# Moving every large tile of a fused two-block kernel onto 512-byte or 1024-byte starts

## The reference

```
h = modulate(rms_norm(x, g_norm1), shift1, scale1)
proj = h @ w_in                                   # 1024 x 3088
...
x = x + (1 + gate1) * (mixed @ w_out)             # 1024 x 1024
u = causal_depthwise_conv(h2 @ w_up, w_conv, b_conv)   # 1024 x 5632
val, gte = split(u)
x = x + (1 + gate2) * ((val * silu(gte)) @ w_down)     # 2816 x 1024
...
def swiglu(h, w_gu, w_down):                      # layers two and three
    gate, up = split(h @ w_gu)
    return (silu(gate) * up) @ w_down
```

## Time and profile before

| | |
|---|---|
| time, median of 3 | 1083.9 us (1081.49 to 1085.06) |
| span of the profiled execution | 1082.7 us; its own time is not listed apart from the three |
| TensorE matmul busy | 1042.9 us, 96% of the span, 9968 matmul records |
| VectorE busy | 734.7 us, 68% |
| ScalarE busy | 562.1 us, 52% |
| transfers | 185.82 MB, 172 GB/s on average |
| granted TensorE clock, mean | 0.985 of full speed |

### The profile page before, as it was taken

One profiled execution on the slowest core, in us unless ns is written; L12 is line 12 of the kernel. 1 busy time (PEld: TensorE's weight loads), 2 busy tenths in 40 slices (PEclk: granted clock), 3 DMA queues, 4 the chain that ended last, 5 costly groups with the idle time before them and its releaser, 6 DMA issues.

```text
span 1082.7 us, 22912 instructions
## 1 busy us (share of the span) xinstructions
PE 1042.9 (96%) x9968; PEld 988.3 (91%) x9968; DVE 734.7 (68%) x1194; ACT 562.1 (52%) x858; POOL 0.9 (0%) x7
## 2 busy tenths in 40 slices
PE   7999999899999999998899999999999999999997
PEld 6798898899999998887779999999989799999996
DVE  3788658799976667887546566566757665556554
ACT  4446374666556448754236444454667655444431
POOL 0000000000000000000000000000000000000000
PEclk8999999899999999999999999999999999999999
DMA  9968455466645653331005555456224435554441
GB/s 348 393 216 312 176 195 204 153 228 237 232 148 176 220 224 118 118 118 42 4 2 170 196 187 187 140 182 222 100 74 155 175 119 195 188 183 149 173 166 39
DMA packets 31236, 185.82 MB, mean 172 GB/s; under 512 B 3472, under 2 KB 4768, under 8 KB 13984
## 3 DMA queue, kind: packets, MB, share of 16 engines
q1 hardware_dynamic: 31136, 184.36, 47.4%
HBM read 183.29 MB, written 1.05 MB: 170 GB/s over the span
## 4 chain that ended last, share of the span: by engine, by line
PE 88%; DVE 5%; ACT 3%; DMA 2%; issue 1%; SPq 1%; DVEq 0%; ACTq 0%
PE banks L361 48%; PE banks L1354 17%; PE banks L341 5%; PE banks L358 2%; PE banks L637 2%; DMA land<-in_mkv_a 1%; DVE wlo L321 1%; PE banks L1538 1%; PE banks L1897 1%; PE banks L1887 1%; PE banks L572 1%; DVE adac L556 1%; PE banks L640 1%; PE banks L1864 1%; DMA raw<-in_w_in 1%
## 5 line engine op out<-in xcount | busy, mean ns | idle before, releaser
L321 DVE TENSOR_TENSOR wlo<-raw,whi 128x2048 fp32r<-128x2048 f32 (+3 forms) x163 | 323.1, 1983 | 172.5 <-ACT whi L306 171.7
L306 ACT ACTIVATE whi<-raw 128x2048 fp32r<-128x2048 f32 (+3 forms) x163 | 270.5, 1661 | 109.3 <-PE banks L1354 78.0
L361 PE MATMUL banks<-h_hi,whi 128*128 128x256 f32 x1376 | 181.1, 283 | 1.3 <-ACT h_hi L987 1.2
L361 PE MATMUL banks<-h_lo,whi 128*128 128x256 f32 x1376 | 179.2, 281 | 0.7 <-DVE h_lo L1062 0.7
L361 PE MATMUL banks<-h_hi,wlo 128*128 128x256 f32 x1376 | 177.4, 281 | 0.0
L361 PEld LDWEIGHTS banks<-h_hi,whi 128*128 128x128 f32 x1376 | 169.1, 189 | 4.7 <-issue 2.5
L361 PEld LDWEIGHTS banks<-h_lo,whi 128*128 128x128 f32 x1376 | 167.4, 187 | 4.1 <-issue 2.6
L361 PEld LDWEIGHTS banks<-h_hi,wlo 128*128 128x128 f32 x1376 | 167.8, 188 | 1.6 <-issue 1.2
L1380 ACT ACTIVATE u<-u 128x256 f32<-128x256 f32 x44 | 18.4, 418 | 128.9 <-DVE u L1434 128.8
L1354 PE MATMUL banks<-m_lo,whi 128*128 128x256 f32 x528 | 75.4, 281 | 0.0
L1354 PE MATMUL banks<-m_hi,wlo 128*128 128x256 f32 x528 | 75.3, 281 | 0.0
(11 more groups left out here) (449 smaller groups left out, 1405.2 us busy)
## 6 DMA issues: line engine op xcount, KB each, us to landing
raw<-in_ada SPq DMA_DIRECT2D x24, 1024.0 KB, 6.2
raw<-in_w_up SPq DMA_DIRECT2D x22, 1024.0 KB, 4.8
raw<-in_a_gu SPq DMA_DIRECT2D x22, 1024.0 KB, 4.8
raw<-in_b_gu SPq DMA_DIRECT2D x22, 1024.0 KB, 4.9
raw<-in_w_in SPq DMA_DIRECT2D x12, 1024.0 KB, 7.1
raw<-in_w_down SPq DMA_DIRECT2D x16, 704.0 KB, 4.1
raw<-in_a_in SPq DMA_DIRECT2D x11, 1024.0 KB, 5.6
raw<-in_a_down SPq DMA_DIRECT2D x16, 704.0 KB, 4.1
```

Of the source, the lines that this page charges most:

```text
L306: act.activation(hi_s[k % NSPLIT][:, 0:w], raw[n % NRAW][:, 0:w], ACT.Copy).then_inc(*hi_made.tick(k))
L321: dve.tensor_tensor(lo_s[s][:, 0:w], raw[n % NRAW][:, 0:w], hi_s[s][:, 0:w].bitcast(F), SUB).then_inc(*lo_made.tick(k))
L361: i_ = pe.matmul(b[0:m, j * T:(j + 1) * T], a[:, kt * step + j * m:kt * step + j * m + m], x[:, kt, :], start=st, stop=sp)
```

## The change

No instruction is added, removed or moved: each engine's list of instructions before and after differs in line numbers alone. What differs is where tiles start. Four pads that nobody reads or writes take up 64, 96, 480 and 992 bytes of a partition, and `one` is allocated behind `masks` instead of ahead of it.

```diff
         vec = sb("vec", [P, NVEC])
         con = sb("con", [P, NCON])
+        sb("pad_low", [P, 16])
         raw = [sb(f"raw{i}", [P, SLOT]) for i in range(NRAW)]
         hi_s = [sb(f"whi{i}", [P, SLOT], R) for i in range(NSPLIT)]
         lo_s = [sb(f"wlo{i}", [P, SLOT], R) for i in range(NSPLIT)]
         X = sb("X", [P, 8, T])
+        sb("pad_high", [P, 120], side="right")
         early = ExitStack()
...
         adac = sb("adac", [P, 2, 2, P])
+        masks = sb("masks", [P, 7, P], R)
         one = sb("one", [P, 1])
-        masks = sb("masks", [P, 7, P], R)
...
         oma = sb("oma", [P, 6])
+        sb("pad_mid", [P, 24])
...
         gdec = sb("gdec", [P, 8], F, sc)
+        sb("pad_mix", [P, 248], F, sc)
         S1 = sb("S1", [P, 2, 4, 256], F, sc)
```

## The result

The changed kernel takes **1098.1 us**, the median of four executions (1097.2 to 1099.5). The kernel before took 1082.7 us beside it (four executions, 1080.9 to 1085.1). The recorded ratio is 1.0131, with a 95% interval from 1.0106 to 1.0156 (the two medians alone divide to 1.0142): slower by 1.3%, where 2.3% faster was forecast, and outside the range.

What follows compares the result with a forecast made beforehand. TensorE, busy 96% of the span, bounds; at 113.3 ns h saves 15.4 us, m 8.5, L358 0.9, others 1.8: 26.6, times 0.96 is 25.5, 1082.7 to 1057.2, forecast 1059 (own range 1054 to 1064; stated range 1046 to 1090).

Steps and rivals of the forecast that it cites:

- nothing changes: Rival for the whole kernel: excess is weight-load handover, addresses do not matter; 1084 us (1081 to 1087), chance 0.17.
- The moving tile: TensorE's matmuls: moving tiles on multiples of 128 bytes allow the quicker pace, 113.3 ns against 116.67 (h) and 118.69 (m).
- The upper bound: Slowest pace allowed for matmuls at the new starts: m's 118.69 ns, for everything.
- The weight load: TensorE's weight loads: 16 or 64 columns also give 117.5 ns, so the excess belongs to the moving side.
- the slower rival: Equal remainders bring moving and weight streams into step, locking all stretches at m's pace: 1088 to 1096 us, chance 0.18.
- Shortening TensorE by 3% leaves both idle: Layer two's up-projection: VectorE, busy 68.69 of 117 us, and ScalarE, 53.57, would not swallow the gain.
- mixed paces: Rival: some matmul stretches lock at 113.3 ns, others at 118.1; 1063 to 1078 us, chance 0.15.
- four fifths fast: Case of the mixed-paces rival with four fifths at the quick pace, over 6,700 matmuls: 1064 us.

Runs made afterwards that it cites:

- one pad of 32 bytes: The kernel before with only h's tiles moved by 32 bytes, making h's difference to the weights 0 modulo 256: 1095.1 us, ratio 1.0109.
- The streams by themselves: Separate kernels, no part of the reference: streams of 32 matmuls at chosen tile starts; 120.0 ns per matmul at difference 0, 113.3 at 192 in the first.
- the three pads: The kernel before plus pads of 96, 32 and 224 bytes, putting all moving tiles 192 from the weights modulo 256: 1069.1 us, ratio 0.9879, lowest median.

## Why the prediction was wrong

**What held.** TensorE is the bound, traffic isn't the excess, and the address reaches the pace: the rival "nothing changes" is refuted by one pad of 32 bytes. VectorE's and ScalarE's times don't see the remainder, float32 records stayed at 216 ns, TensorE's idle time at 40 us, and the paces of h and m did become equal.

**The step that failed** is "The moving tile". I wrote that the `mm` tiles "are the only moving tiles on a multiple of 128 bytes", and that this "is what seems to allow the quicker pace". They differed from the others in a second way that the same table of starts shows: they stood 192 bytes from the weights modulo 256, and no other tile did. The streams by themselves show that this was it: both tiles moved together kept 120.0 at six other starts. The forecast then took "only multiples of 128 are like the new starts" to pick 113.3 out of bounds from 108 to 118.69. The upper bound was wrong too: 120.0 stood in no row of before, since none of its tiles had difference 0.

**The step that led there** is "The weight load". From equal paces at 16, 64 and 128 weight columns I concluded that "the excess belongs to the moving side", and used it against the slower rival, "so the two streams hardly meet". Those rows have different moving tiles at different differences, and the 16-column loads step by 64 bytes, so that their difference changes with each block: the comparison held nothing fixed. In the streams by themselves the width does matter: at difference 0, 128 columns give 120.0 in every one of 50 stretches (119.7 to 120.0), and 16 columns 113.3 in five of six (116.7 once). In the kernel after, 64 columns give 113.8 where 128 give 120.0. That 16 and 64 columns both came to 117.5, between h's 116.67 and m's 118.69, was chance as far as these runs tell.

**The rival that was right.** "Equal remainders bring the streams into step" named the mechanism and even the 32 bytes between h and `whi`; I gave it 0.18. It priced the pace by the slowest row at hand, 118.69, and so said 1093. With 120.0 its own sum is 3.33 x 4560 = 15.2 for h and 1.31 x 1584 = 2.1 for m, 17.3 us, and x 0.96 makes 16.6: 1099.3 from the 1082.7 of the kernel before, against the measured 1098.1.

**The size of the gain** was too large even where the pace mostly came true. Of my 25.5 us the three pads gave 17.7 in the profiled execution and 13 by the ratio, a third to a half less. "Shortening TensorE by 3% leaves both idle" was judged by busy time, 69 and 54 of 117 us, where the spacing of the splits, 5.58 us against TensorE's 5.60, would have told that there was hardly any slack. And I took the quick pace as held by all matmuls, although had two paces at one address; my "mixed paces" rival, 1063 to 1078, describes what the best kernel does, though not the change that was made. (Its case of four fifths fast comes to 1065.5 by its own terms, 2.84 ns x 6734 x 0.96 = 18.4 us below 1083.9, and not to 1064.)

## What to carry to other kernels

Where long streams of rounded-float32 matmuls bind, print the start of each moving tile minus the start of the weight tile, modulo 256: with 128 weight columns and 256 moving ones, among multiples of 32, 0 and 96 were the worst (120.0) and 192 the best (113.3, or 117.8), and equalizing alignments is the way to get 0. The differences can be set with a pad of 32 to 224 bytes, and it is worth a run of streams by themselves first, since at 384 and 512 columns the order turns round. Before pricing a quicker engine, measure the spacing of its suppliers' output, not their busy share.

## What the runs showed of the hardware that was not expected

- The optimum depends on the number of moving columns. At 512 columns differences 0 and 256 give 226.7 ns and 128, 192 and 480 give 232.3 to 233.5; at 384 columns 173.3 at 0, 256 and 480, 176.1 to 176.7 at 128 and 192; at 128 columns about 111.7 at all of them, hardly quicker than 256 columns take.
- A moving tile 4 bytes past the weight tile's start gave 123.3 ns, with 232 bytes (122.4 and 123.4) the slowest of all that were tried at these widths. Streams that alternated between differences 0 and 192 from one matmul to the next took 116.7 to 119.9.
- At difference 0 it made no difference whether the weight tile stepped by 512 or 1024 bytes (120.0), so that suspicion of the "nothing changes" rival has no support.
- The Trainium skill (SBUF — State Buffer, "Who interferes with whom") gives TensorE two independent read ports, one for the moving operand and one for the weight load. The runs show that they aren't independent in effect: the pace follows the distance between the two tiles and the width of the load. What meets there, a bank, a buffer or an arbiter, no run here shows; that the pace repeats after 256 bytes is all that is measured.
- What picks the pace at the beginning of a stretch is known only by example. A kernel that holds every stretch of h at 113.3 wasn't found.
